# Three transformer blocks on one Trainium2 core: new start addresses for the weight ring, the work area and the ring of high parts

## What is computed

```python
D_MODEL = 2048; BATCH = 1; SEQ = 256; DEPTH = 1
...
x = first_block(x, ...)    # rms norm, w_in, latent attention + RWKV-7 scan in both directions, gates, w_out
x = second_block(x, ...)   # w_in, conformer conv + pooling + Fourier mix, w_out, layer norm, gated FFN (5632)
x = third_block(x, ...)    # adaptive norm (w_ada), w_in, stick-breaking + sparse attention, w_out, conv FFN (5504)
```

## The kernel before

| operand | before | after the change |
|---|---|---|
| `ring`, `ring_parts` | 128 / 640 | 256 / 768 |
| `ring_hi1` (first block) | 480 / 992 | 512 / 0 |
| `ring_hi` (afterwards) | 160 / 672 | 256 / 768 |
| chunks in `work`: h, x, mix, hid, p (high and low) | 480 | 512 |
| `hs_hi` (third block) | 736 | 512 |
| `o3_lo` (third block, output projection) | 608 | 640 |
| `resid` | 96 | 224 |

## Time and profile before

### The profile page before, as it was taken

One profiled execution on the slowest core, in us unless ns is written; L12 is line 12 of the kernel. 1 busy time (PEld: TensorE's weight loads), 2 busy tenths in 40 slices (PEclk: granted clock), 3 DMA queues, 4 the chain that ended last, 5 costly groups with the idle time before them and its releaser, 6 DMA issues.

```text
span 3725.6 us, 63401 instructions
## 1 busy us (share of the span) xinstructions
PE 3562.8 (96%) x26060; PEld 3360.3 (90%) x26060; DVE 2231.9 (60%) x3036; ACT 1407.4 (38%) x1686; POOL 76.1 (2%) x155
## 2 busy tenths in 40 slices
PE   8998899999999999989999999998998899999998
PEld 8996688888888886789999999988988899999998
DVE  7775455555446569765555554545566677777544
ACT  5441132332320000554444433335355444445443
POOL 0001100000000100000000000000000000000000
PEclk9998999999999999989999999999999999999999
DMA  8657511111137984435555555543442455555554
GB/s 315 253 187 316 217 62 60 48 48 59 62 135 277 382 335 149 172 125 183 188 182 190 181 193 192 193 169 127 160 158 97 154 183 189 182 190 181 192 192 147
DMA packets 91728, 654.13 MB, mean 176 GB/s; under 512 B 10177, under 2 KB 10817, under 8 KB 13122
## 3 DMA queue, kind: packets, MB, share of 16 engines
q1 hardware_dynamic: 74736, 540.05, 40.1%
q0 software_dynamic: 14256, 103.82, 7.1%
q10 hardware_dynamic: 2594, 8.15, 0.6%
HBM read 649.88 MB, written 2.10 MB: 175 GB/s over the span
## 4 chain that ended last, share of the span: by engine, by line
PE 86%; DVE 7%; DMA 3%; ACT 3%; issue 1%; ACTq 0%; DVEq 0%
PE ps L442 19%; PE ps L444 19%; PE ps L443 19%; PE ps L414 8%; PE ps L603 6%; DMA work<-in_ada 3%; PE ps L677 2%; PE ps L665 2%; PE ps L473 1%; DVE work L1589 1%; PE ps L488 1%; DVE ring_parts L1574 1%; PE ps L721 1%; PE ps L712 1%; ACT work L1218 1%
## 5 line engine op out<-in xcount | busy, mean ns | idle before, releaser
L1574 DVE TENSOR_TENSOR ring_parts<-ring,ring_hi 128x1024 fp32r<-128x1024 f32 x810 | 976.5, 1224 | 787.9 <-ACT ring_hi L1054 777.8
L1054 ACT ACTIVATE ring_hi<-ring 128x1024 fp32r<-128x1024 f32 x810 | 852.8, 1061 | 1085.9 <-PE ps L444 1072.2
L443 PE MATMUL ps<-h_lo,ring_hi 128*128 128x256 f32 x2624 | 733.5, 280 | 0.0
L442 PE MATMUL ps<-h_hi,ring_hi 128*128 128x256 f32 x2112 | 596.4, 282 | 16.3 <-DVE ring_parts L1574 11.9
L444 PE MATMUL ps<-h_hi,ring_parts 128*128 128x256 f32 x2112 | 593.2, 281 | 0.0
L443 PEld LDWEIGHTS ps<-h_lo,ring_hi 128*128 128x128 f32 x2624 | 494.5, 188 | 1.3 <-issue 1.2
L442 PE MATMUL ps<-x_hi,ring_hi 128*128 128x256 f32 x1664 | 467.3, 281 | 5.8 <-DVE x_lo L1596 4.5
L444 PE MATMUL ps<-x_hi,ring_parts 128*128 128x256 f32 x1664 | 467.5, 281 | 0.0
L443 PE MATMUL ps<-x_lo,ring_hi 128*128 128x256 f32 x1664 | 463.6, 279 | 0.0
L442 PEld LDWEIGHTS ps<-h_hi,ring_hi 128*128 128x128 f32 x2112 | 398.3, 189 | 19.3 <-DVE ring_parts L1574 13.5
L444 PEld LDWEIGHTS ps<-h_hi,ring_parts 128*128 128x128 f32 x2112 | 399.1, 189 | 0.0
(11 more groups left out here) (422 smaller groups left out, 5418.9 us busy)
## 6 DMA issues: line engine op xcount, KB each, us to landing
ring<-in_weights SPq DMA_DIRECT2D x511, 1024.0 KB, 4.8
work<-in_ada POOLq DMA_DIRECT2D x96, 1024.0 KB, 8.9
work<-in_c_row POOLq DMA_DIRECT2D x3, 1024.0 KB, 5.2
resid<-in_lora ACTq DMA_DIRECT2D x9, 256.0 KB, 2.6
resid<-in_x SPq DMA_DIRECT2D x4, 512.0 KB, 6.3
resid<-in_x ACTq DMA_DIRECT2D x1, 2048.0 KB, 14.6
out<-work SPq DMA_DIRECT2D x4, 512.0 KB, 2.9
con<-in_const ACTq DMA_DIRECT2D x1, 1536.0 KB
```

The source lines that it names most:

```text
L442: mm(o, w_hi[:, k, cols], hi(kc), start=(kc == 0 and m % 2 == 0), stop=False, skip_group_check=True)
L443: mm(o, w_hi[:, k, cols], lo(kc), start=False, stop=False, skip_group_check=True)
L1054: A(high_ring(n)[:, 2 * (e % 2) + half, :], ring[:, n % RING, half * (SLOT // 2):(half + 1) * (SLOT // 2)], ACT.Copy)\
L1574: tt(lo, x, high_ring(n)[:, e % 4, :].bitcast(F32), ALU.subtract).then_inc(S("lo_ready"), 1)
```

## The change

Two pads (`pad_to`) move `ring` from byte 1152 to 1280 and the work area from byte 70112 to 71168; `con`, `par`, `resid`, `mod`, `red` and `std` move by the 128 bytes of the first pad. Within the work area `HI` moves from offset 35504 to 35264, and the views that stand at 64 words past a multiple of 256 (`hs_hi` and the attention scratch around it) move by 192 words. The area is 80 words shorter. No instruction is added, removed or moved; only addresses in their operands differ. In the first block `ring_hi1` keeps its offset, a multiple of 256 words, as the features have.

```diff
--- before.py
+++ after.py
@@ -23,7 +23,7 @@
 KPS = 4
 SLOT = KPS * COLS
 RING = 4
-WORK = 39600
+WORK = 39520
 HEADS = 8
 RANK = 512
 NOPE, ROPE = 128, 64
@@ -211,6 +211,13 @@
         return sems[name]
 
 
+    def pad_to(at, residue, step):
+
+        words = (residue - -(-at // 32) * 32) % step // 4
+        if words:
+            sb(f"pad{at}", [P, words])
+
+    pad_to(nc.sbuf_base, 256, 1024)
     ring_at = -(-nc.sbuf_base // 32) * 32
     ring = sb("ring", [P, RING, SLOT])
     ring_parts = nc.alloc_sbuf_tensor_at("ring_parts", [P, RING, SLOT], F32R, offset=ring_at)
@@ -220,7 +227,9 @@
     MOD = sb("mod", [P, 96])
     RED = sb("red", [P, 2, T])
     STD = sb("std", [P, 2, T])
+    pad_to(nc.sbuf_base, 512, 1024)
     work_at = -(-nc.sbuf_base // 32) * 32
+    assert (ring_at % 1024, work_at % 1024) == (256, 512)
     W = sb("work", [P, WORK])
     PS = ctx.enter_context(nc.psum_tensor("ps", [P, 8, 512], F32))
 
@@ -322,7 +331,7 @@
     GU, GU2, GU3 = w(30720, 4, T), w(31744, 4, T), own("gu", 32768, 4, T, dt=F32)
     P2, P2_HI, P2_LO = w(33792, 2, T), own("p_hi", 34304, 2, T), own("p_lo", 33792, 2, T)
     BROW = w(20736, 2 * COLS)
-    HI = own("ring_hi", 35504, 4, SLOT // 2)
+    HI = own("ring_hi", 35264, 4, SLOT // 2)
 
 
     Q_SB, K_SB, V_SB = w(4096, 8, T), w(6144, 8, T), w(8192, 2, WIDTH)
@@ -332,14 +341,14 @@
     ROT = CON[:, N_3:N_3 + 4 * T].rearrange("p (c t) -> p c t", t=T)
     TURN, TURNI, ANG = w(30720, 4, T), w(30720, 4, T).bitcast(I32), w(31744, 4, T)
     TURN_IX, TURN_DS = w(8192, 4, T), w(17472, 4, T)
-    REL = w(25664, 4, TRI)
-    LG, PTR = [w(25664, 4, TRI), w(21568, 4, TRI)], [w(27200, 4, TRI), w(23104, 4, TRI)]
+    REL = w(25856, 4, TRI)
+    LG, PTR = [w(25856, 4, TRI), w(21760, 4, TRI)], [w(27392, 4, TRI), w(23296, 4, TRI)]
     SCORE, LEFT, SBIAS = w(29760, TRI), w(30144, TRI), w(30528, TRI)
     TOP, SM3 = w(30912, 8), w(30920, 64)
     O3, O3_LO = w(31008, DC, T), own("o3_lo", 31008, DC, T)
     SQ3 = w(15424, DC, T)
     NORM3 = w(4096, DC, T)
-    HS_HI = own("hs_hi", 21568, DC, T)
+    HS_HI = own("hs_hi", 21760, DC, T)
     HID3_HI, HID3_LO = own("hid3_hi", 4096, FF3_CHUNKS, T), own("hid3_lo", 15360, FF3_CHUNKS, T)
     H3_HI, H3_LO = own("h3_hi", 26624, DC, T), own("h3_lo", 0, DC, T)
     UP3 = w(30720, 8, T + 2)
```

## The result

The changed kernel takes 3762.89 us (median of 4 runs, 3759.16 to 3764.7), the kernel before 3725.02 us (median of 4 runs, 3722.5 to 3728.68). The ratio is 1.0100 (95% interval 1.0082 to 1.0117): slower by 1.0%, 38 us, where I forecast no difference and gave a range up to 3750.

The account below looks back on a forecast made before the run. The prediction took TensorE's queue of matmuls, at 117.8 ns from start to start, as the bound. All terms were put at zero, summing to 0 us on 3726.9 us, so it forecast 3726 us, range 3620 to 3750.

Parts of the forecast that it names:

- Plain float32 products: L414, L603, L473: a weight load 10 ns quicker or slower stays hidden under the stream at 215.4 ns; zero.
- The split on DVE: Splitting on ACT and DVE, L1054 and L1574: their waiting covers any change of some ns; zero, 16 us without that cover.
- The transfers: Loads of `w_ada` land on rounder addresses in the moved work area; zero, with 9 us either way.
- The refuting test: Second block's timeline rows: forecast is wrong if the pace differs from 117.8 ns by more than 0.4 ns.
- the term of the split products: 17,264 of 18,672 products get moved distances; taken as zero, between -98 us and +71 us.
- The twelve distances: Start distances modulo 1024, even and odd tiles, in three stages of the old layout: all at one pace, 117.8 ns.
- my count: Split products: 2 x 704 in the first block keep their distances, 17,264 of 18,672 are moved.
- Rival 2: Split products: tiles now symmetric, 256 below and above the chunk, so both collide and pace rises; 3739 to 3797 us; chance 0.14.
- lower price: Slower split products: 0.7 ns on each of 18,672, taken from group `misc` at 118.5 ns; 13 us, giving 3739.
- upper bound: Slower split products: 3.8 ns on each of 18,672, from the product with 512 moving columns; +71 us, giving 3797.
- Rival 1: Split products: read interference of 6 to 10 ns goes, so faster; 3707, 3628 or as low as 3578 us; chance 0.20.

Follow-up runs that it names:

- experiment 1: TensorE-only program instead of the kernel, 51 groups of 96 products at chosen start addresses, some with tiles 1024 bytes apart: 120.0 ns with both distances 0, 117.9 at (0, 160).
- experiments 9 and 10: Changed kernel with distances (64, 192), first block (0, 192): 3663.54 us; the same with o3 moved so the third block's output projection has (64, 192): 3661.49 us.
- experiment 2: TensorE-only program instead of the kernel, 306 groups of 72 products, mostly a grid of high and low distances in 16-byte steps: 113.3 to 124.5 ns.

## Why the prediction was wrong

**What held.** TensorE bounds the kernel, and a change of its pace goes into the time in full: 2.2 ns on 17,904 products, 39 us, against a measured 38. Plain float32 products did not move (82.89 us twice). Their pace is 215.8 ns and not 215.4, since that piece of the chain begins a little behind the first product's start; the sum does not turn on it. The split on DVE took 1224 ns in the mean as before and that on ACT 1057 where it was 1061, and their waiting covered what there was. The transfers gained nothing that can be put down to the addresses. The refuting test that I named, a pace more than 0.4 ns from 117.8, is what the timeline shows.

**The step that failed** is the term of the split products, put at zero where it measured 2.2 ns on each of 17,904, 39 us: "Between these I take zero, since the rows of this very product are nearest: 192 lies only 64 bytes from 256 [...] 0 and 512 are the far end". It fails three times over.
- *The twelve distances were few.* The period is 256 bytes. The tiles of one chunk start 512 bytes apart and so share one distance, and what I counted as even and odd is one case. What remains are (0, 160), (192, 160) and, in one stage, a part at 64. The low ring had 160 in all rows. The old layout had made two experiments and a small third, not twelve.
- *The first block was no sample of the new distance.* I took its high ring at 0 and 512, with a pace of 117.8, as a test of the far end. It was a test of 0 for one ring beside 160 for the other. Only the pair tells: (0, 160) and (192, 0) run at 117.8, (0, 0) at 120.0, and undoing either edit alone takes the loss back. For the same reason my count was off: the first block's high ring products, which I left out as not moved, slowed too.
- *Near is not alike.* The pace doesn't fall off with distance, it jumps; (0, 16) is at 117.8 and (0, 0) at 120.0. "A cost that fell with distance would have told these two apart" is true, and the cost isn't of this kind.

Rival 2 had the direction and nearly the place: slower, in all stages, without another engine. Its lower price of 0.7 ns was a third of the 2.2 measured, and its upper bound of 3.8 from the 512-column product did hold it; I drew the range at 3750 by the lower price. That the bound held was luck: it rests on the 512-column product as a piece of the same interference, and under the change this product got 2.6 ns quicker while the 256-column product got 2.2 slower. Its mechanism, one tile in two that collides, is refuted: in experiment 1, groups whose tiles do not alternate by 512 run at 120.0 at every multiple of 256 as well. Rival 1 named something real: the 117.8 had slack, and the pairs of experiments 9 and 10 take 4.4 of the 5.7 ns that the earlier trace rows allowed. It was only not this change that won it.

The rule that I weighed, the Trainium skill's "TensorE: Matmul & The Clock Gate", Part 2, "Step-by-step: what each phase is for", says that weights and the moving operand come through two independent read ports of SBUF and that loading weights takes no read bandwidth from the running matmul. By it the start addresses cannot matter. Experiment 1 has nothing but these two reads and gives 117.8 or 120.0 ns by the addresses alone, and experiment 2 113.3 to 124.5, so here the measurement decides against drawing that conclusion from the rule. The same page's 109.2 ns ("Back-to-back issue gap") was reached by no pair; the best was 113.3. The page gives its formula for a single matmul by itself and says that in a stream of weight loads and matmuls both set the spacing, so as a price for rival 1 it was too low.

**What stays open.** Why these distances cost what they do. The runs show that the two address streams of TensorE's operands are enough, that their distances count and not where they stand, and that both matter together. The period of 256 bytes rests on the groups with both rings at one distance and on the kernel's own layouts; the grid does not reach beyond 256. Whether it is the reads that meet, or something in how the two are timed against each other, no run here separates. Neither is it known why a pair with several rhythms takes the one or the other, nor why 512 columns have another order than 256. A first block at 113.3 was not tried: its high ring lies between features that are still in use.

## What to carry to other kernels

When a kernel is a dense stream of weight load and matmul, the start addresses of the operands are a parameter of it like a tile size, and worth a sweep with TensorE alone: the sweep takes one short run, repeats the kernel's paces to 0.1 ns, and here led to 1.6% less time with no instruction changed. Sweep the combinations that occur together and visit each several times, in random order, since the effect is one of pairs and some pairs are fast only sometimes, and for each number of moving columns, since what is slowest for 256 was fastest of four for 512. And before taking "it is alike at twelve places" as evidence, reduce the twelve by every period that the layout can have: an experiment that the old layout made is worth only as many points as are different in what matters.

## What the runs showed of the hardware

- 256-column float32r products with 128x128 weights, at the granted clock of 1.00, run at 113.3 to 124.5 ns from start to start, with nothing changed but the distances of the operands' starts; where 256 bytes were added to both distances, the pace stayed, but for (64, 64), which has two. Rounder is not better: both rings level with the features gives 120.0, and 232 of the 256 pairs of the grid are faster.
- With 512 moving columns it is the other way round: level gives 226.7 ns, a distance of 128 gives 232.3 and one of 160 gives 233.3; in the kernel 229.3 fell to 226.7 with the change.
- The pace often locks to one value, such as 848 cycles for three products before the change and 864 after it, and holds it to 0.1 ns over the 380 and 260 us of the windows.
- Some pairs have more than one pace: (64, 64) gave 113.3 or 117.8 in one program, and a kernel with it spread over 56 us from run to run, where (64, 192) spread over 4.
